# Seven-product pairs with two of their four weight sums made by accumulating transfers, and the norm factor moved to the down result

## The reference

```
def _swiglu(h, w_gate, w_up, w_down):
    return (silu(h @ w_gate) * (h @ w_up)) @ w_down

x = x + 0.5 * _swiglu(_rmsnorm(x, ffn1_norm[l]), ffn1_w_gate[l], ffn1_w_up[l], ffn1_w_down[l])
```

## Time and profile before

| what | value |
|---|---|
| median of 3 runs | 3309.1 us (3308.97 to 3309.43) |
| the profiled execution | 3310.0 us |
| its span, first to last instruction | 3308.2 us |
| mean granted TensorE clock | 0.993 |
| TensorE, VectorE, ScalarE, GpSimd busy | 3125.8, 2197.6, 1384.5, 1213.2 us |
| data moved | 289.17 MB, mean 87 GB/s |

### The profile page before, as it was taken

One profiled execution on the slowest core, in us unless ns is written; L12 is line 12 of the kernel. 1 busy time (PEld: TensorE's weight loads), 2 busy tenths in 40 slices (PEclk: granted clock), 3 DMA queues, 4 the chain that ended last, 5 costly groups with the idle time before them and its releaser, 6 DMA issues.

```text
span 3308.2 us, 48205 instructions
## 1 busy us (share of the span) xinstructions
PE 3125.8 (94%) x17808; PEld 2629.3 (79%) x17808; DVE 2197.6 (66%) x3151; ACT 1384.5 (42%) x2328; POOL 1213.2 (37%) x899
## 2 busy tenths in 40 slices
PE   7898999989999898999989999999999999999999
PEld 6888876788887888876688887768788886688887
DVE  6849578685876949578695875456747555567474
ACT  5434336443434424336442433464424335444242
POOL 4636427562645626417562642023000213220003
PEclk9999999999999999999999999999999999999999
DMA  4245341223232233331223233212333322123332
GB/s 118 84 130 140 91 121 46 77 84 102 84 93 79 80 106 90 88 82 45 77 83 102 83 94 104 77 39 71 98 93 95 107 75 61 45 77 105 88 100 82
DMA packets 528498, 289.17 MB, mean 87 GB/s; under 512 B 13630, under 2 KB 520225, under 8 KB 528314
## 3 DMA queue, kind: packets, MB, share of 16 engines
q1 hardware_dynamic: 523706, 273.40, 28.9%
q0 software_dynamic: 4608, 13.30, 1.4%
HBM read 284.38 MB, written 10.02 MB: 89 GB/s over the span
## 4 chain that ended last, share of the span: by engine, by line
PE 50%; POOL 17%; issue 17%; DVE 9%; ACT 4%; DMA 1%; DVEq 0%; ACTq 0%; POOLq 0%; SPq 0%
PE bank L2332 29%; PE bank L2350 5%; POOL ws_raw L859 4%; POOL gated L864 3%; POOL s_two L849 3%; POOL s_two L846 3%; PE bank L2637 3%; POOL ws_raw L855 2%; PE bank L2747 2%; PE bank L2367 2%; PE bank L2435 2%; PE bank L2789 2%; PE bank L2812 1%; PE bank L2570 1%; ACT w_hi L1031 1%
## 5 line engine op out<-in xcount | busy, mean ns | idle before, releaser
L1031 ACT ACTIVATE w_hi<-w_raw 128x1024 fp32r<-128x1024 f32 (+2 forms) x311 | 359.0, 1155 | 1002.6 <-PE bank L2332 614.0
L2385 PE MATMUL bank<-h_hi,ws 128*128 128x256 f32 x2560 | 507.6, 291 | 127.1 <-DVE prod L1834 84.4
L1614 DVE TENSOR_TENSOR w_lo<-w_raw,w_hi 128x1024 fp32r<-128x1024 f32 (+2 forms) x279 | 423.7, 1519 | 287.6 <-ACT w_hi L1031 287.5
L2385 PEld LDWEIGHTS bank<-h_hi,ws 128*128 128x128 f32 x2560 | 415.5, 194 | 155.6 <-DVE prod L1834 97.6
L2332 PE MATMUL bank<-h_hi,w_hi 128*128 128x512 f32 (+1 forms) x1140 | 452.3, 397 | 13.8 <-DVE w_lo L1614 10.0
L2332 PE MATMUL bank<-h_hi,w_lo 128*128 128x512 f32 (+1 forms) x1140 | 444.6, 390 | 0.0
L2332 PE MATMUL bank<-h_lo,w_hi 128*128 128x512 f32 (+1 forms) x1128 | 439.9, 390 | 0.0
L2385 PE MATMUL bank<-h_lo,ws 128*128 128x256 f32 x1280 | 365.6, 286 | 0.0
L2385 PE MATMUL bank<-t_hi,ws 128*128 128x256 f32 x1920 | 361.2, 284 | 2.7 <-ACT gate_sum L1229 2.7
L2332 PE MATMUL bank<-act_hi,w_hi 128*128 128x512 f32 x836 | 325.3, 389 | 0.0
L2332 PE MATMUL bank<-act_hi,w_lo 128*128 128x512 f32 x836 | 325.2, 389 | 0.0
(11 more groups left out here) (392 smaller groups left out, 6890.9 us busy)
## 6 DMA issues: line engine op xcount, KB each, us to landing
w_raw<-in_ffn_w_down_dram SPq DMA_DIRECT2D x64, 704.0 KB, 4.6
w_raw<-in_ffn_w_in_dram SPq DMA_DIRECT2D x88, 512.0 KB, 3.8
raw_g<-in_ffn_w_gate_dram SPq DMA_DIRECT2D x80, 512.0 KB, 4.8
raw_u<-in_ffn_w_up_dram SPq DMA_DIRECT2D x71, 512.0 KB, 3.9
w_raw<-in_ffn_w_out_dram SPq DMA_DIRECT2D x32, 704.0 KB, 4.4
w_raw<-in_w_in_dram SPq DMA_DIRECT2D x34, 512.0 KB, 3.8
w_raw<-in_a_w_qkv_dram SPq DMA_DIRECT2D x24, 512.0 KB, 3.7
w_raw<-in_w_out_dram SPq DMA_DIRECT2D x16, 512.0 KB, 3.7
```

The costliest lines, as they stand in the source:

```text
L1031: nc.scalar.activation(split_home(c)[0][:, 0:nk, 0:cols], raw[c % 2][:, 0:nk, 0:cols], ACT.Copy).then_inc(hi_ready, 1)
L1614: nc.vector.tensor_tensor(w_low[:, 0:nk, 0:cols], raw[c % 2][:, 0:nk, 0:cols], w_high[:, 0:nk, 0:cols].bitcast(f32), ALU.subtract).then_in ...
L2385: mm = nc.tensor.matmul(dst, w, v, start=(first and k == 0 and n == 0), stop=(k == KH - 1 and n == 2), skip_group_check=True)
```

## The change

In fast pairs, four things.

1. **Signs.** The first token sum is taken the other way round, so that weight sums need additions only: `up0 + up1`, `gate0 + (up0 + up1)`, `gate0 + up0`, and `gate1 + (gate0 + up0 + up1)`. The up result comes out negative; the minus goes into the down result's factor, and into the plain pairs' product.
2. **Two sums by transfers.** SP loads `up0` straight into `s_two[:, 1]` (`fast_one`), and GpSimd issues a transfer of `up1` that adds onto it (`first_two`). SP loads `gate0` instead of `up0` into the first half of `raw_u`, and GpSimd issues a transfer of `up0` that adds onto that (`third_sum`). GpSimd itself makes only the sums for P6 (`first_two`) and P3 (`last_sum_of`). `s_two` still has one buffer: `fast_one` waits for `sums_low` of the pair before (its reader) and for `last_sum_of` of the pair before.
3. **Factor.** `gate_scale` and L1854 are gone. The down result is multiplied by -0.5 and `rstd` into `down_t`, and a second VectorE instruction adds that to `xres`.
4. **Order.** The third and fourth sum are rounded and reduced separately. On VectorE `up_cross` comes before `sums_low` of the next pair, and `product` is in two parts. On ScalarE silu comes before the copy of P1, and in a first half the rounding of the first fast pair comes before the second silu.

```diff
+            def fast_up(name, hf, j, gate, w):
                 if prior is not None:
-                    sp.wait_ge(s_made, 4 * of_pair(name, *prior) + 3)
+                    sp.wait_ge(low_part, 4 * of_pair(name, *prior) + 3)
                     sp.wait_ge(lo_ready, c + 30 * prior[0] + 2 * prior[1] + 2)
+                sp.dma_start(raw_up(name, j)[:, 0:KH, :], gate[:, 0:KH, cols]).then_inc(three_in[p], 16)
+                sp.dma_start(raw_up(name, j)[:, KH:KT, :], w[:, KH:KT, cols]).then_inc(u_full[p], 16)
+            def fast_one(name, hf, j, w):
+                n = of_pair(name, hf, j)
+                if j == FAST_FROM[hf] and hf == 0:
+                    sp.wait_ge(rstd_ready, ROOT[name] + 1)
+                if n:
+                    sp.wait_ge(low_part, 4 * (n - 1) + 2)
+                    sp.wait_ge(s_made, 2 * (n - 1) + 2)
+                sp.dma_start(s_two[:, 1, :].rearrange("p (k f) -> p k f", k=KH),
+                             w[:, 0:KH, (hf * FH + j) * P:(hf * FH + j + 1) * P]).then_inc(one_in, 16)
...
                 for j in range(FAST_FROM[0], FH):
                     fast_gate(name, 0, j, gate)
-                    fast_up(name, 0, j, up)
+                    fast_up(name, 0, j, gate, up)
+                    fast_one(name, 0, j, up)
...
+            def third_sum(name, hf, j):
+                pool.wait_ge(three_in[p], 16 * LOADED[name, hf, j])
+                pool.dma_start(raw_up(name, j)[:, 0:KH, :], up_weights(name)[:, 0:KH, cols],
+                               accum_op=ALU.add).then_inc(three_made[p], 16)
+            def first_two(name, hf, j):
+                pool.wait_ge(one_in, 16 * (n + 1))
+                pool.dma_start(s_two[:, 1, :].rearrange("p (k f) -> p k f", k=KH), up_weights(name)[:, KH:KT, cols],
+                               accum_op=ALU.add).then_inc(one_made, 16)
+                pool.wait_ge(one_made, 16 * (n + 1))
+                pool.wait_ge(g_full[j % 2], 16 * LOADED[name, hf, j])
+                if n:
+                    pool.wait_ge(low_part, 4 * (n - 1) + 2)
+                nc.gpsimd.tensor_tensor(s_two[:, 0, :], s_two[:, 1, :],
+                                        raw_g[j % 2][:, 0:KH, :].rearrange("p k f -> p (k f)"), ALU.add).then_inc(s_made, 1)
+            def last_sum_of(name, hf, j):
...
+                    pool.wait_ge(prod_done, product_count(name, hf, j - 1, "P3"))
+                pool.wait_ge(s_made, 2 * n + 1)
+                nc.gpsimd.tensor_tensor(ws_raw[:, 5, 1, :], s_two[:, 0, :],
+                                        raw_g[j % 2][:, KH:KT, :].rearrange("p k f -> p (k f)"), ALU.add).then_inc(s_made, 1)
-            def gate_scale(name, hf, j):
-                pool.wait_ge(silu_ready, FF[name] + FH * hf - CONV_FF[name] + 1 + j)
-                nc.gpsimd.tensor_tensor(gated[:, :], gated[:, :], rstd[:, :], ALU.mult).then_inc(gate_ready, 1)
...
                     for j in range(FAST_FROM[hf], FH):
...
+                        last_sum_of(name, hf, j)
                         if rows:
                             copy_bias_row()
                         if j + 1 < FH:
-                            weight_sums(name, hf, j + 1, False)
+                            third_sum(name, hf, j + 1)
+                            first_two(name, hf, j + 1)
...
+                    if how == "scaled":
+                        nc.vector.scalar_tensor_tensor(down_t[b][:, :, :], got, -0.5, rstd[:, :].rearrange("p (o n) -> p o n", o=1),
+                                                       ALU.mult, ALU.mult).then_inc(down_scaled, 1)
+                        dve.wait_ge(down_scaled, n + taken + 1)
+                        ins = nc.vector.tensor_tensor(xres[:, DS(n, 1), :], down_t[b][:, :, :], xres[:, DS(n, 1), :], ALU.add)
...
                         if j > j0:
                             gate_last(hf, j - 1)
-                            sums_low(name, hf, j, True)
+                        three_low(name, hf, j)
+                        if j > j0:
+                            product_last(hf, j - 1)
                         gate_first(hf, j)
+                        four_low(name, hf, j)
+                        if j > j0:
+                            product_first(hf, j - 1)
                         if more:
                             raw_low(name, hf, j + 1)
-                        last_low(hf, j)
                         if j > j0:
                             act_low(a0 + j, j - 1)
+                        last_low(hf, j)
+                        up_cross(hf, j)
                         if more:
-                            sums_low(name, hf, j + 1, False)
+                            sums_low(name, hf, j + 1)
-                        up_cross(hf, j)
```

More of the change, by code:

```diff
@@ L302, in program @@
         norm_t = [put(f"norm_t{i}", [P, T], prob_at + 4 * i * T) for i in range(4)]
+        down_t = [put(f"down_t{i}", [P, 1, T], prob_at + 12 * i * T) for i in range(2)]
         gate_sum = [put(f"gate_sum{i}", [P, T], prob_at + 4 * T * (1 + i)) for i in range(2)]
@@ L678, in fast_ff @@
                         fast_gate(name, 1, 0, gate)
-                        fast_up(name, 1, 0, up)
+                        fast_up(name, 1, 0, gate, up)
+                        fast_one(name, 1, 0, up)
                 for j in range(1, FH):
                     fast_gate(name, 1, j, gate)
-                    fast_up(name, 1, j, up)
+                    fast_up(name, 1, j, gate, up)
+                    fast_one(name, 1, j, up)
                 for n in range(KT):
@@ L852, in weight_sums @@
+            def last_sum_of(name, hf, j):
+                n, c = of_pair(name, hf, j), BASE[name] + 30 * hf
+                if j == FAST_FROM[hf]:
                     pool.wait_ge(mm_done, c + (4 if hf == 0 else 0))
                 else:
-                    pool.wait_ge(prod_done, product_count(name, hf, j - 1, "P7"))
-                nc.gpsimd.tensor_tensor(ws_raw[:, 4, 1, :], gate[0], up[0], ALU.subtract).then_inc(s_made, 1)
-                if not first:
                     pool.wait_ge(prod_done, product_count(name, hf, j - 1, "P3"))
-                pool.wait_ge(s_made, 4 * n + 2)
@@ L1738, in act_low, with output_gemm @@
                                         act_hi[:, DS(jj, 1), :].bitcast(f32), ALU.subtract).then_inc(act_ready, 1)
[L1740 removed]
+            def output_gemm(c, how, name, halves=False, fast=None, taken=0):
                 def take(c, n, j=0):
@@ L1770, in output_gemm @@
                     raw_low(fast, 1, 0)
-                    sums_low(fast, 1, 0, False)
+                    sums_low(fast, 1, 0)
                     take(c + KT - 1, KT - 1)
@@ L1897, in gated_ff @@
                         small_values()
-                    output_gemm(down, "half", name if hf else None, fast=None if hf else name)
+                    output_gemm(down, "scaled", name if hf else None, fast=None if hf else name,
+                                taken=KT * (HALVES * FAST[name] + hf))
             def conv_ff(name):
```

150 lines of the change are left out of this document (74 added, 76 removed).

## The result

The changed kernel takes 3458.4 us (median of four runs, 3448.7 to 3465.9) against 3309.3: a ratio of 1.045, 95% interval 1.042 to 1.048. The forecast of 3286 was wrong, the sign too. The profiled run took 3455.9 us (span 3453.8, against 3308.2 before).

The account below looks back on a forecast made before the run. The kernel was taken as bound by TensorE, losing 1.9 us per pair to waits for VectorE. Gains of 31.6 us less 7.5 given back net 24.1, taking 3310.0 to 3285.9, forecast as 3286, range 3200 to 3430.

Parts of the forecast that it names:

- The mechanism: Loop over s_two's single buffer, 11.76 us, outlasts TensorE's 10.2 and sets the pair; TensorE waits before the third product.
- the plain load: SP's 256 KB load into s_two, in the loop: 3.3 us to land, bounds 2.8 and 4.0.
- the engines have room: DMA engines can carry 1.75 MB per pair instead of 1.0, judged from a share of 0.31.
- the slow rival: Adding transfer into s_two takes longer, making the kernel slower than before: 3358 us at 5.4, 3502 at 7.4; chance 0.38.
- The adding transfer: GpSimd-issued 256 KB transfer adding onto s_two, in the loop: 4.4 us, bounds 3.1 and 7.4.
- break-even of 4.73: Adding-transfer time in us at which the net gain over the kernel before is zero.
- The bias rows: First stage's second half, sharing the adding transfers' queue: 0.5 us more in nine loops, 4.5 us.
- The lag: Added after a half's loops because late sums_low delays VectorE's closing of the pair before: 1.0 us, bounds 0 and 1.98.
- The first sums of a stage: First fast pair's s_two sums, after its transfers, addition, rounding and remainder: ready at 663.6 in the second such stage.
- VectorE's load: VectorE's work per pair falls from 11.1 us to about 8, as GpSimd's additions stretch its instructions less.
- GpSimd kept from issuing by VectorE: Rival: VectorE holds up GpSimd's transfer issue by up to 1.98 us per loop, giving 3429 us; chance 0.04.
- The short rival: Transfers land in 2.8 and 3.1 us, the loop is 10.0, TensorE's 10.2 rules: 3194 us; chance 0.22.

Follow-up runs that it names:

- e1_plain: Changed kernel with the adding transfer into s_two made a plain copy, so the up sum lacks its first half: 3357.9 us, ratio 1.015.
- e2_third_late: Changed kernel with the third sum's adding transfer issued right after that of s_two, not before the wait for the plain load: 3341.9 us, ratio 1.010.
- e10_plain_late: Changed kernel with the adding transfer into s_two made a plain copy and the third sum's adding transfer issued after it: 3249.6 us, ratio 0.982.
- e4: Changed kernel with GpSimd adding the up halves of s_two itself; the third sum keeps its adding transfer: 3212.4 us, ratio 0.971.
- e7: Changed kernel with the third sum added by GpSimd right after that of s_two, whose adding transfer is kept: 3419.6 us, ratio 1.033.
- e5: Kernel before with only the factor moved to the down result; all weight sums stay GpSimd's, no transfer adds: 3225.4 us, ratio 0.974.
- e9: Changed kernel with GpSimd adding s_two's up halves and the third sum's adding transfer issued after GpSimd's two s_two additions: 3281.2 us, ratio 0.991.
- e3: Changed kernel with a second buffer for the up sum of s_two in three of the four stages: 3305.4 us, ratio 0.999.

## Why the prediction was wrong

The loop in parts, from start to start in the timelines, means over 51 loops of stages 2 to 4 (all but the first of each second half). The addition, ScalarE and VectorE terms have their hand-over in them:

| | forecast | changed | e1_plain | e2_third_late | e10_plain_late |
|---|---|---|---|---|---|
| `sums_low` to SP's issue | 0.05 | 0.05 | 0.12 | 0.12 | 0.12 |
| plain load | 3.35 | 4.92 | 4.85 | 3.42 | 3.38 |
| second transfer | 4.45 | 4.99 | 3.60 | 4.79 | 3.51 |
| addition | 1.36 | 1.40 | 1.42 | 1.39 | 1.40 |
| ScalarE | 1.12 | 1.09 | 1.09 | 1.13 | 1.13 |
| VectorE | 1.43 | 1.35 | 1.36 | 1.36 | 1.42 |
| loop | 11.76 | 13.80 | 12.46 | 12.21 | 10.96 |

- **The mechanism was right.** `s_two`'s one buffer sets the pair, TensorE waits in front of the third product for it, the pair moves with each term of the loop, and 72 us per 1 us of loop held: by the table 72 x 1.34 = 96 for e1's 100.5, 72 x 1.59 = 114 for e2's 116.5, 72 x 2.84 = 204 for e10's 208.7. Of the 246 us between the changed kernel and e4, the 72 intervals hold 223.
- **The step that failed is the plain load, 3.3 us with an upper bound of 4.0.** It took 4.9. I put half a microsecond on it for both neighbours at once, by the rate at which two plain loads slow each other. A transfer that adds, issued on GpSimd's queue 1.2 us earlier, delays it by 1.5: e2 and e7 show it from two sides, and the six early loops a third time. I had costed the adding transfer of `s_two` and never asked what the other one does to its neighbours; the bound was then too tight as well. Behind it stands a reading that does not hold: "the engines have room" at a share of 0.31, and "two thirds idle" against the slow rival. That was a mean over a whole pair. In the 4 us in which the plain load is under way the share is 1.15, which is 4.6 us of work for all the engines, and by the estimate under e1 close to half of that is the other adding transfer's.
- **The adding transfer, 4.4, took 5.0**, within its bounds and past the break-even of 4.73. The rival that the forecast ranked highest on the other side was right in kind, but it alone gives 3286 + 72 x 0.54 = 3325. The step from a plain best case of 3.1 missed that GpSimd's issue grows too, from 0.78 to 1.28. The price also came from copies, and in e1 copies on GpSimd's queue went in far fewer packets than adding transfers.
- **The bias rows, 0.5 per loop, cost 0.8** beyond the other stages in the changed kernel (14.6 against 13.8), 1.9 in e2.
- **The lag, 1.0, is 2.12**, within 0.01 in all 17 loops of the second stage in which TensorE waits. The chain `sums_low`, L1874, L1877, silu, L1260 is fixed work in order, not a chance collision. Twice per stage, 8 x 1.1 = 9 us. The first sums of a stage come 0.8 later than forecast, 3 us.
- **Together:** 62 x 2.04 + 10 x (14.6 - 12.26) + 9 + 3 = 162, so 3448 of the profiled 3456. The 8 left I can't place; the stretches of TensorE's lower clock are a candidate, mostly hidden in its own waits, and were not tested alone.
- **VectorE's load** fell as forecast in the changed kernel (7.9 us per pair, and 0.68 for L1860). But the gain that the forecast put down to that is not what e5 shows: there VectorE works as long as before, and the 84 us won lie near the 78.3 in which it no longer stands behind L864, the second of the two reasons that the forecast named. The two instructions on a down result cost too little to see beside it.
- **GpSimd kept from issuing by VectorE** did not occur: L867 took 1.27 and 1.28 at minimum and median, with VectorE's tensor_tensor instructions beside it. The Trainium skill (SBUF — State Buffer, Who interferes with whom) states that GpSimd is locked out by VectorE's two-port modes and that tensor_tensor has none; the trace agrees.
- **The short rival** rested on 2.8 and 3.1. In e2 and e7 the plain load landed in 3.1; the adding one never took less than 4.4. The Trainium skill's figure for a GpSimd-issued transfer (DMA: Bandwidth & Descriptors, Anatomy of one DMA), 2.6 for 256 KB, was too short: the plain one on GpSimd's queue took at best 3.2, median 3.4.

## What to carry to other kernels

Before an addition is moved into a transfer, ask whether the transfer stands in a loop closed by a single buffer. There an adding transfer of 256 KB in the place of one addition of 1.3 us cost 246 us; outside the loop, the same trick lost nothing and won 9 us at best. When two new transfers run near each other, price each on the other, and look at what is queued behind whoever waits for them: an issue moved by a few us was worth 116 us one way (e2) and cost 69 the other (e9). Whether the DMA engines have room is read over the few microseconds of the transfer, not from the mean of a stage. A part of a change that wins and one that loses are worth timing apart: the factor on the down result alone gave 2.6%.

## What the runs showed of the hardware

- A transfer that adds, 256 KB, takes 4.4 us at best and 4.8 in the median on GpSimd's queue; the same one copying takes 3.2 and 3.4. GpSimd is held 1.28 us to issue it, 0.78 for the copy. It goes in 528 packets, the copy in 80; by an estimate from the queue's share it is 2.15 us of work for all sixteen engines, the copy 0.9 (pages of before, changed, e1 and e4).
- Behind another adding transfer it takes 5.7 (e3), and a plain load that SP issues 1.2 us after one lands in 4.7, not 3.1. The DMA share is 1.15 in 4 us of such a flight, though 0.64 over the half stage.
- TensorE's granted clock has two levels in the changed kernel, 1.00 and 0.50 (1.2 GHz). In the first half of the second stage it stayed at 1.00 after pauses of 1.46, 1.78 and 1.80 us and stood at 0.50 for 3 to 7 us from around the end of pauses of 3.43, 4.44, 5.58 and 5.80. The length of the pause alone does not tell: in the second half it fell to 0.50 after one of 2.14 and stayed up after ones of 2.91 and 2.96. At the lower level it is 0.22 us from one matmul to the next, where 0.12 is usual. A window and the timeline of the changed kernel:
```profile
711.30:714.00 2.70, 2.68 (x12) 2.68 (x13) 2.66 (x4) 1.95 (x3) 1.27 (x1) 0.50 0.67 195
```
```profile
711.32 0.58 PE L2441 MATMUL bank<-t_hi,ws 128*128 128x256 f32 x1 [5.80 <-ACT gate_sum L1260]
711.70 0.41 PE L2441 MATMUL bank<-t_lo,ws 128*128 128x256 f32 x1
711.92 0.41 PE L2441 MATMUL bank<-t_hi,ws 128*128 128x256 f32 x1
```
